# A hybrid decoder step on one core: the first scan tile's silu and split put off, x1's squares folded further, x's roots broadcast by DMA, B's rows in another PSUM bank

## The reference

```python
def trunk(x, ...):
    mix, h_new, sbuf, cbuf = mixer(rmsnorm(x, norm_pre_mix), ...)
    x = x + rmsnorm(mix, norm_post_mix)
    hid = jnp.square(jax.nn.relu(rmsnorm(x, norm_pre_mlp) @ w_up))
    x = x + rmsnorm(hid @ w_down, norm_post_mlp)

def mixer(u, h0, ...):
    z, xbc, dt_raw, glu = split(u @ w_in)
    xs, B, C = split(silu(conv4(xbc)))
    y, h_new = ssd_scan(xs, softplus(dt_raw), A, B, C, h0)   # chunks of 128 tokens
    ssd_out = group_rmsnorm((y + d_skip * xs) * silu(z)) * ssd_norm_w
    v = glu[:D] * sigmoid(glu[D:])
    conf_out = silu(layernorm(conv31(v)) * conf_norm_w + conf_norm_b)
    mix = concat([ssd_out, conf_out]) @ w_out
```

## Time and profile before

| | |
|---|---|
| median of 3 runs | 1778.71 us (1777.17 to 1778.88) |
| the profiled execution | 1777.03 us, its span 1775.4 us |
| PE matmul busy | 1757.6 us, 99% |
| PE weight load busy | 1733.9 us, 98% |
| DVE / ACT / POOL busy | 1079.3 / 760.3 / 442.3 us |
| granted TensorE clock | 0.999 of full |
| DMA | 285.31 MB, 161 GB/s mean |
| chain that ended last | PE 96%, DVE 2%, ACT 1% |

### The profile page before, as it was taken

How to read it: one execution, slowest core, us unless ns; L and a number is a source line. 1 busy time by engine, 2 the same in 40 slices (tenths; PEclk the granted TensorE clock), 3 DMA queues, 4 the chain that set the end, 5 groups by cost and what they waited for, 6 DMA issues and landing times.

```text
span 1775.4 us, 34636 instructions
## 1 busy us (share of the span) xinstructions
PE 1757.6 (99%) x13159; PEld 1733.9 (98%) x13159; DVE 1079.3 (61%) x1977; ACT 760.3 (43%) x1088; POOL 442.3 (25%) x332
## 2 busy tenths in 40 slices
PE   8999999999999999999999999999999999999998
PEld 7999999999998999999899999999999999999998
DVE  5587867999778788955865333444344443344444
ACT  7443435555347566523543333343333333333442
POOL 1577676776651112133000000000000000000132
PEclk9999999999999999999999999999999999999999
DMA  8665554555556777754344544445444444444442
GB/s 246 197 182 158 148 157 137 152 146 154 155 152 182 231 226 223 236 162 150 99 148 155 165 153 144 142 142 164 153 144 155 142 143 156 138 157 157 150 142 84
DMA packets 292264, 285.31 MB, mean 161 GB/s; under 512 B 12390, under 2 KB 287630, under 8 KB 291296
## 3 DMA queue, kind: packets, MB, share of 16 engines
q1 hardware_dynamic: 268008, 257.31, 47.6%
q10 hardware_dynamic: 22512, 19.23, 3.4%
q0 software_dynamic: 1648, 7.43, 1.3%
HBM read 268.06 MB, written 17.31 MB: 161 GB/s over the span
## 4 chain that ended last, share of the span: by engine, by line
PE 96%; DVE 2%; ACT 1%; DMA 0%; issue 0%; SPq 0%; DVEq 0%; ACTq 0%
PE ps L1829 29%; PE ps L1830 29%; PE ps L1831 29%; PE ps L2078 1%; PE ps L2094 1%; PE ps L2119 1%; PE ps L2113 1%; PE ps L2155 1%; PE ps L1887 1%; PE ps L2157 1%; PE ps L2156 1%; PE ps L1889 1%; PE ps L1888 1%; DMA xn<-in_x_prompt 0%; DVE wlo L1235 0%; DVE mix L1696 0%
## 5 line engine op out<-in xcount | busy, mean ns | idle before, releaser
L1829 PE MATMUL ps<-ahi,whi 128*128 128x320 f32 x2304 | 717.9, 312 | 0.0
L1831 PE MATMUL ps<-ahi,wlo 128*128 128x320 f32 x2304 | 711.9, 309 | 0.0
L1830 PE MATMUL ps<-alo,whi 128*128 128x320 f32 x2304 | 711.8, 309 | 0.0
L703 ACT ACTIVATE whi<-raw 128x1024 fp32r<-128x1024 f32 x463 | 478.2, 1054 | 397.2 <-PE ps L1831 380.5
L1235 DVE TENSOR_TENSOR wlo<-raw,whi 128x1024 fp32r<-128x1024 f32 x344 | 423.5, 1254 | 233.6 <-ACT whi L703 231.7
L1829 PEld LDWEIGHTS ps<-ahi,whi 128*128 128x128 f32 x2304 | 432.6, 188 | 2.1 <-issue 0.5
L1830 PEld LDWEIGHTS ps<-alo,whi 128*128 128x128 f32 x2304 | 432.7, 188 | 0.5
L1831 PEld LDWEIGHTS ps<-ahi,wlo 128*128 128x128 f32 x2304 | 432.5, 188 | 0.0
L1829 PE MATMUL ps<-hhi,whi 128*128 128x320 f32 x1016 | 314.3, 309 | 0.0
L1831 PE MATMUL ps<-hhi,wlo 128*128 128x320 f32 x1016 | 313.9, 309 | 0.0
L1830 PE MATMUL ps<-hlo,whi 128*128 128x320 f32 x1016 | 313.9, 309 | 0.0
(11 more groups left out here) (317 smaller groups left out, 1550.2 us busy)
## 6 DMA issues: line engine op xcount, KB each, us to landing
raw<-in_w_in SPq DMA_DIRECT2D x144, 512.0 KB, 3.7
raw<-in_w_up SPq DMA_DIRECT2D x128, 512.0 KB, 4.3
raw<-in_w_down SPq DMA_DIRECT2D x128, 512.0 KB, 4.5
raw<-in_w_out SPq DMA_DIRECT2D x64, 512.0 KB, 4.1
h<-in_state_ssm ACTq DMA_DIRECT2D x16, 512.0 KB, 4.9
out<-hout SPq DMA_DIRECT2D x16, 512.0 KB, 3.8
wgt<-running_sums ACTq DMA_DIRECT2D x16, 320.0 KB, 5.5
x_transposed<-xt ACTq DMA_DIRECT2D x1, 2560.0 KB, 13.6
```

The source lines that it names most:

```text
L703: act.activation(whi[:, kq, :, 0:width], raw[:, kq, :, 0:width], ACT.Copy).then_inc(hi_done, 1)
L1829: pe.matmul(out, wh, hi[:, kk, :], start=(kk == 0), stop=False)
L1830: pe.matmul(out, wh, lo[:, kk, :], start=False, stop=False)
L1831: last = pe.matmul(out, wl, hi[:, kk, :], start=False, stop=(kk == NT - 1))
```

## The change

Four edits, and a wait or two that go with them.

1. At T = 0 ACT no longer does `conf_silu(3)` before `decay(0)`: it copies `h0t` first, then `decay(0)`, and `conf_silu(3)` follows the padding for T = 1. DVE's `conf_act(3)` moves from behind the first split of weights to behind the gate of T = 0.
2. B's three tiles and the product of B and C go to bank 7. TensorE waits for the copy `btok` before the fifth transpose of h0 (the first that writes to bank 7), no longer before x's.
3. The roots `sx` are stored to DRAM by three small DMAs from POOL in the GLU stage, and one DMA from POOL, behind the last h store, broadcasts them to `xrow` on all partitions. `diag`, the three products and their semaphores are gone; `scale_x` reads `xrow`.
4. DVE folds `sqx[2:4]` onto `sqx[0:2]`, and TensorE sums two tiles.

```diff
-        diag = place("diag", [P, 3, P], at=sm + 2560)
+        xrow = place("xrow", [P, TOK], at=sm + 2560)
...
+        roots = nc.dram_tensor("token_roots", (1, TOK), F32, kind="Internal").ap()
...
             glu(1)
             pool.dma_start(s_cc[0, :, 0:HALO - DS, :], state_conf[0, :, DS:HALO, :]).then_inc(old_rows, 16)
+            pool.wait_ge(sx_done, 3)
+            for c in range(3):
+                lo, hi = c * P, min((c + 1) * P, TOK)
+                pool.dma_start(roots[0:1, lo:hi].rearrange("o p -> p o"), sx[0:hi - lo, c:c + 1]).then_inc(roots_stored, 16)
             with pool.Fori(2, 8) as i:
...
             pool.wait_ge(hout_out, 16 * NT)
+            pool.wait_ge(roots_stored, 16 * 3)
+            pool.dma_start(xrow[:], roots.to_broadcast([P, TOK])).then_inc(xrow_in, 16)
             v = st.inc(pool.memset(acc2[:], 0.0))
...
                     if j == 0:
                         act.wait_ge(bt_trans, i + 1)
-                        act.activation(btok[:], ps[:, 4, :].rearrange("p (c n) -> p c n", c=4), ACT.Copy
+                        act.activation(btok[:], ps[:, 7, :].rearrange("p (c n) -> p c n", c=4), ACT.Copy
                                        ).then_inc(btok_ready, 1)
-                    if first:
-                        conf_silu(3)
-                    decay(T)
+                    if not first:
+                        decay(T)
                     act.wait_ge(h0_trans, T + 1)
                     act.activation(h0t[:, 0:4, :], ps[:, 6, :].rearrange("p (b n) -> p b n", b=4), ACT.Copy)
                     act.activation(h0t[:, 4:8, :], ps[:, 7, :].rearrange("p (b n) -> p b n", b=4), ACT.Copy
                                    ).then_inc(h0t_ready, 1)
-                    if not first:
+                    if first:
+                        decay(T)
+                    else:
                         act.wait_ge(hnew_done, T)
...
                         if j == 3:
                             pad_b(i + 1)
+                    if first:
+                        conf_silu(3)
...
                     ahead(Q_WC, i, 0 if first else 2 * j + 1)
                     if first:
-                        conf_act(3)
                         ahead(Q_WC, i, 1)
...
                     dve.wait_ge(g_done, T + 1)
+                    if first:
+                        conf_act(3)
...
                 dve.wait_ge(hout_out, 16 * NT)
-                for c in range(3):
-                    last = dve.tensor_scalar(diag[:, c, :], ident[:], sx[:, c:c + 1], None, ALU.mult)
-                last.then_inc(sdiag_done, 1)
...
-                dve.tensor_tensor(x, x, ps[:, 5, 0:TOK].unsqueeze(1).to_broadcast([P, 4, TOK]), ALU.mult
+                dve.tensor_tensor(x, x, xrow[:].unsqueeze(1).to_broadcast([P, 4, TOK]), ALU.mult
...
             dve.wait_ge(xr_in, 16)
-            dve.wait_ge(s_mm, 1)
+            dve.wait_ge(xrow_in, 16)
...
             dve.wait_ge(dve_step, v)
-            dve.sem_inc(acc_done, 1)
+            dve.tensor_tensor(sqx[:, 0:2, :], sqx[:, 0:2, :], sqx[:, 2:4, :], ALU.add).then_inc(acc_done, 1)
...
-                        pe.transpose(ps[:, 4, k * P:(k + 1) * P], btiles[c], ident[:])
-                    pe.matmul(ps[:, 4, P:2 * P], xb[:, NT + i, 0:P], xb[:, NT + GROUPS + i, P:SEQ],
+                        pe.transpose(ps[:, 7, k * P:(k + 1) * P], btiles[c], ident[:])
+                    pe.matmul(ps[:, 7, P:2 * P], xb[:, NT + i, 0:P], xb[:, NT + GROUPS + i, P:SEQ],
...
                     last.then_inc(cb_done, 1)
-                    pe.wait_ge(btok_ready, i + 1)
...
                 for b in range(NB):
+                    if j == 0 and b == 4:
+                        pe.wait_ge(btok_ready, i + 1)
                     last = pe.transpose(ps[:, 6 + b // 4, (b % 4) * P:(b % 4 + 1) * P], h0[:, j % 2, b, :],
...
-            pe.wait_ge(sdiag_done, 1)
-            pe.wait_ge(rooted, 6)
-            for c in range(3):
-                last = pe.matmul(ps[:, 5, c * P:min((c + 1) * P, TOK)], ones[:], diag[:, c, 0:min(P, TOK - c * P)],
-                                 start=True, stop=True)
-            last.then_inc(s_mm, 1)
...
                 pe.wait_ge(acc_done, 2)
-                for n in range(4):
-                    last = pe.matmul(ps[:, 5, 0:TOK], mean1[:], sqx[:, n, :], start=(n == 0), stop=(n == 3))
+                for n in range(2):
+                    last = pe.matmul(ps[:, 5, 0:TOK], mean1[:], sqx[:, n, :], start=(n == 0), stop=(n == 1))
```

More of the change, by code:

```diff
@@ L293, in build @@
             sem("x1_done"))
-        sdiag_done, s_mm, q1s_done = sem("sdiag_done"), sem("s_mm"), sem("q1s_done")
+        roots_stored, xrow_in, q1s_done = sem("roots_stored"), sem("xrow_in"), sem("q1s_done")
         mix_tile = sem("mix_tile")
```

## The result

The changed kernel takes 1784.44 us (median of 6 runs, 1783.81 to 1786.90) against 1777.94 for the kernel before in the same session: ratio 1.004, 95% interval 1.003 to 1.0051, so 6.5 us slower where 2.3 faster was forecast. Its profiled execution took 1784.67 us with a span of 1783.0 (before: 1777.03 and 1775.4); the two spans are compared here. The runs of most kernels here lie in two clusters some 1.5 us apart (the kernel before: 1777.0 to 1777.7 and 1778.5 to 1779.0), so half a per mille between two medians can be a matter of how many runs fell in each.

What follows compares the result with a forecast made beforehand. TensorE, busy 99% of 1775.4 us, was taken as the bound. Gains 0.40 + 0.87 + 0.68 + 0.35 = 2.30 us, off 1778.3, gave 1776.0 us; 8 in 10 from 1773.4 to 1778.2.

Steps and rivals of the forecast that it cites:

- part 3: x's roots: three products leave TensorE's stream, gain 0.68 us (0.59 to 0.83); the added DMA issues are covered.
- The 320 four-byte writes have 640 us to land: Root stores in the GLU stage: they land long before their broadcast is needed, so cost nothing.
- POOL's issues: GLU stage: three DMA issues at 0.55 us each, 1.65 in all, delay POOL's splits within 3.0 us of cover, cost 0.
- Rival (b): GLU stage: POOL's issues cost by element, 12.3 us, TensorE waits 9.3; 7.0 us slower, 1785.3; chance 0.05.
- a stretch removed from TensorE is worth its length: Whole kernel: the clock stays at its top tenth throughout, so time removed from TensorE counts in full.
- Part 1: First scan tile: reordered silu and split let TensorE's granule (kq 3) at T=1 start at 563.78, not 564.18; gain 0.40 us.
- the 0.2 us wait: T=1, before L2071: what is left of TensorE's 2.54 us wait once y_read comes at 560.80.
- the 1.8 us wait: T=1, before granule kq 3: new TensorE wait on act_ready, as the last quarter's split now stands behind y_read.
- Part 2: B's rows in bank 7: the wait before L2071 on ACT's btok copy goes; gain 0.87 us (0 to 1.2).
- three times 0.29: Bank 7's sum: 0.29 us waited before L2071, gained in three of four groups, the first spent in part 1.
- Part 4: x1's squares: two fewer products save 0.96 us, of which 0.35 remains as gain (minus 0.2 to 0.96).
- the wait forecast on wlo: Granule behind the splits at 903.34: TensorE, moved up by 0.96, would stop 0.6 us for wlo.

Runs made afterwards that it cites:

- e2: On e1: three 512-byte row stores from POOL to a DRAM scratch where the root stores stood; 1777.55 us, ratio 0.9998 against the kernel before.
- e4: Changed kernel with the 1.4 MB copy of old rows moved behind POOL's GLU loop, root stores left in place; 1776.19 us, ratio 0.9992 against the kernel before.
- f1: On e1: three column stores of 128 four-byte elements lying 512 bytes apart, beside the copy; 1777.50 us, ratio 0.9998 against the kernel before.
- g3: On e1: one column store of 128 adjacent four-byte elements right behind the copy of old rows; 1785.91 us, ratio 1.0044 against the kernel before.
- e3: Changed kernel with its three root stores moved behind POOL's GLU loop, away from the 1.4 MB copy; 1776.30 us, ratio 0.9991 against the kernel before.
- f2: Changed kernel with the three root stores issued ahead of the copy of old rows; 1782.81 us, ratio 1.0041 against the kernel before.
- h1: Changed kernel with the three root stores issued by ScalarE into its own queue, the copy left in place; 1783.68 us, ratio 1.0033 against the kernel before.
- g1: f4 with VectorE's second split put back ahead of the eight state updates; 1773.71 us, ratio 0.9977 against the kernel before.
- f3: e4 with the first scan tile in its old order, conf_silu(3) and conf_act(3) back where they were; 1776.11 us against e4's 1776.19.
- g2: g1 with ScalarE's four casts of the gated tiles behind its second weight split in groups 3 and 4; 1773.12 us, ratio 0.9971 against the kernel before.
- f4: On e4: VectorE's first tile reordered, bm ahead of the wait for the exponential, second split last; 1780.59 us, ratio 1.0011 against the kernel before.
- e1: Changed kernel with the roots made by diag and three products again, no root stores or xrow; 1777.53 us, ratio 0.9999 against the kernel before.

## Why the prediction was wrong

**What failed** is one sentence of part 3: "The 320 four-byte writes have 640 us to land." It asked who waits for the stores, and not what they do to the transfers in flight beside them. A few sentences earlier the same step had reckoned POOL's issues right: 1.70 us for three (1.65 forecast), the first late split done in time, no stop at 96. Rival (b) had the slower side, and nearly its number (1785.3), by luck: its mechanism was POOL's issue time, and by e2 that costs nothing.

What takes its place: column stores whose elements lie side by side hold the loads for some 4 us alone (e4, covered) and beside the copy until a weight load lands after 18.59 us (uncovered by 6.66). A smaller step failed with it: "a stretch removed from TensorE is worth its length" reckons with a full clock, and behind the stop 1.7 us more were lost at half clock. The runs show that the uncovered stall needs elements close together (f1 against g3) and the copy in flight (e3, e4), and neither a place behind the copy (f2), nor GpSimd's queue (h1), nor three stores (g3, though three stop TensorE for longer).

By what rule the memory serves such writes, no run shows. The Trainium skill (DMA: Bandwidth & Descriptors, Specifications) says that a transfer under 512 bytes is done as a read-modify-write. Adjacent elements might then queue for one and the same piece of memory, which fits f1 and g3 and is shown by neither; but the page's rule holds for f1's writes as well, and those cost nothing; the measurement decides.

**Part 1, first tile: 0.40 forecast, 0 measured.** On the path of the last quarter each step held but one. With the 8.96 taken off, L2122 started at 554.80 (forecast 554.81), y_read came at 560.74 (560.80), the quarter's split began at 561.36 (561.30). The split itself was mis-sized: rows of before made it 2.34, after it took until 573.07:

```profile
569.73 0.49 DVE L1622 TENSOR_TENSOR zg<-ysum,zg 128x320 f32<-128x320 f32 x1
570.32 0.83 DVE L1505 CAST ahi<-cf 128x1280 fp32r<-128x1280 f32 x1
571.25 1.82 DVE L1507 TENSOR_TENSOR alo<-cf,ahi 128x1280 fp32r<-128x1280 f32 x1
```

POOL squares the tile's gated product just then (L635, 1.17 us from 570.55), because the split now stands behind the gate and not ahead of it. Ahead of it, in g1, the same instruction takes 1.49. These 0.33 us, and 0.06 by which the split began late, make 564.16 for the granule (573.12 less 8.96) where 563.78 was forecast and 564.18 stood before; f3 is in keeping with the zero. TensorE's own arrival was wrong as well, and hidden: forecast free at 560.60, it reached x's transposes of T=1 only at 561.95 (570.91 less 8.96), at half clock before, so the 0.2 us wait there was none and the 1.8 us wait behind them 0.85. The Trainium skill (SBUF — State Buffer, SBUF: two separate sides) says that a DVE operation with two SBUF inputs and a GpSimd operation that reads SBUF exclude each other; the trace agrees in kind: the two overlap for 0.47 us (571.25 to 571.72) and the split takes 0.33 longer, and e4 has the same 1.82 at the same overlap.

**Part 2, bank 7: 0.87 forecast, 0.28 measured.** The waits went as forecast in all groups: the second group's transposes, 0.41 behind L2063 in the earlier trace rows, stand 0.17 behind now (0.12 forecast):

```profile
606.28 0.33 PE L2071 MATMUL ps<-xb,pad 128*128 128x64 f32 x2
606.45 0.39 PE L2078 MATMUL ps<-ident,xb 128*128 128x128 f32 x2
```

But in the third and fourth group 0.28 of it is gone one tile later (8.39 to 8.67 in the table), where y_read hangs on ACT and not on TensorE. There ACT's chain starts where it did (its btok copy of the third group is 8.68 late, 652.09 against 643.41), so what TensorE gained by the bank it soon waits for again. The step "three times 0.29" left that wait out. g2 moves four casts out of the chain and gets more back than was lost (0.40 at T=9, 0.76 at T=13).

**Part 3, products: 0.68 forecast, 0.67 measured** (8.68 at T=13, 8.01 ahead of x1's squares). The three products were the right price; it was the other side of the exchange that cost.

**Part 4, squares: 0.35 forecast, 0.45 measured** (8.01 to 7.56). Between, TensorE stood 1.08 earlier, and the wait forecast on wlo is there, 0.47 against 0.6:

```profile
893.09 1.24 PE L2215 MATMUL ps<-sqx,mean 128*128 128x320 f32 x4
893.92 0.55 PE L1837 MATMUL ps<-ahi,whi 128*128 128x320 f32 x1
...
912.39 0.41 PE L1837 MATMUL ps<-ahi,whi 128*128 128x320 f32 x1 [0.47 <-DVE wlo L1245]
```

So the four parts give 0 + 0.28 + 0.67 + 0.45 = 1.40 us in the changed kernel's trace, of 2.30 forecast. e3 and e4, where nothing is held up, stand 2.2 and 2.3 under the kernel before by their medians, but these medians lie in different clusters: within the lower one e4 has 1776.0 and the kernel before 1777.2, 1.2 apart, and by the spans it is 1.1. The sum was right to about a microsecond; the sign was wrong by what the new stores did to the transfers beside them.

## What to carry to other kernels

Reckon a new transfer by what else is in flight with it, not only by its own due time: columns of adjacent four-byte elements, covered when alone, made a large memory-to-memory copy twice as long and the loads beside it up to four times. Rows of 512 bytes (e2), elements 512 bytes apart (f1), or a time when no large transfer runs (e3, e4) cost nothing; only the last was tried with the real roots. Before a step is put off, follow the queue that waits for it to its end: f4's late split held its own reader for 2.44 us, and VectorE for 5.8 behind a store that merely stood behind the split's reload.

## What the runs showed of the hardware that was not expected

The half clock. Nine kernels have the changed kernel's first tile (it and e1, e2, e3, e4, f1, f2, g3, h1), and all nine show 3.4 us at half clock behind its first or its second stop. Four kernels without that order do not: before (stops of 1.53 and 2.54 us), f3 (1.81 and 2.54), g1 and g2 (0.63 and 0.91 the longest). f4, whose stops are 2.44 and 3.89 us, has 6.8 us that begin within the second. In the changed kernel:

```profile
563.76 0.71 PE L2122 MATMUL ps<-bm,xdd 32*128 32x256 f32 x8 [1.93 <-issue]
...
573.12 0.42 PE L1837 MATMUL ps<-ahi,whi 128*128 128x320 f32 x1 [0.85 <-DVE alo L1507]
```

```profile
565.00:569.00 4.00, 4.00 (x37) 3.86 (x27) 3.97 (x13) 4.00 (x9) 0.00 (x0) 0.57 0.70 220
```

Here the slow stretch comes out of the next stop, which is 0.85 us and not the 1.8 forecast, so it costs nothing. So it is in e1, e2 and e4 (stops of 0.85 to 0.99). In e3, f1, f2, g3 and h1 the slow stretch falls behind that stop, which is then 1.94 or 1.95 us; in e3:

```profile
564.31 0.64 PE L1837 MATMUL ps<-ahi,whi 128*128 128x320 f32 x1 [1.94 <-DVE alo L1507]
```

The products from here on are 0.27 apart, and e3's profiled span is 1.5 us longer than e4's. That is also the distance of the two clusters: e3's and f1's profiled runs (1777.43, 1779.09) lie in their kernels' upper clusters, those of e1, e2 and e4 in the lower. g1 and g2, whose traces have no half clock, have one cluster only (9 runs within 0.5 us, 7 within 0.4). So where the half clock falls probably makes the clusters of these kernels; for the kernel before and f3, which have an upper cluster too, no trace of an upper run was taken, and it stays open. Why 1.93 us of rest is followed by half clock and 1.81 is not, no run here tells: the order of the work around them differs too.
